# One-hots from tile 54 with a row chunk to each pair, and gelus and gates moved in larger pieces, in the expert stage of a hybrid decoder step

## The reference, cut to what matters

```python
def one(xb):
    qh = (xb @ wq).reshape(PEER_BLOCK, PEER_HEADS, 2, PEER_DQ // 2)
    s1 = jnp.einsum('nhd,kd->nhk', qh[:, :, 0], subkeys[0])
    s2 = jnp.einsum('nhd,kd->nhk', qh[:, :, 1], subkeys[1])
    v1, i1 = lax.top_k(s1, PEER_TOPK)
    v2, i2 = lax.top_k(s2, PEER_TOPK)
    cand = v1[..., :, None] + v2[..., None, :]
    sc, ci = lax.top_k(cand, PEER_TOPK)
    e = i1[ci // 16] * 128 + i2[ci % 16]
    g = jax.nn.softmax(sc, axis=-1)
    a = jax.nn.gelu(jnp.einsum('nd,nhkd->nhk', xb, u[e]))
    return jnp.einsum('nhk,nhkd->nd', g * a, v[e])
```

## Time and profile before

| | us |
|---|---|
| median of 3 runs (lowest to highest) | 2361.18 (2359.29 to 2371.97) |
| the profiled execution's own time | 2364.91 |
| its span | 2363.3 |
| PE busy | 2133.0 (90%) |
| DVE busy | 1359.9 (58%) |
| POOL busy | 546.1 (23%) |
| ACT busy | 360.4 (15%) |
| U pass, first product to last group | 955.0 to 1619.6 |
| V pass, first product to last | 1632.5 to 2244.8 |

### The profile page before, as it was taken

The page is one execution under the profiler, slowest core; times in us unless marked ns, Lnnn a source line. Parts: engine busy times, 40 slices in busy tenths (PEclk is TensorE's granted clock), DMA queues, the critical chain, the costliest instruction groups (busy, mean ns, idle before and its releaser), DMA issues. The chain is left out here.

```text
span 2363.3 us, 24834 instructions
## 1 busy us (share of the span) xinstructions
PE 2133.0 (90%) x8879; PEld 1588.1 (67%) x8879; DVE 1359.9 (58%) x2817; ACT 360.4 (15%) x743; POOL 546.1 (23%) x516
## 2 busy tenths in 40 slices
PE   6958989967999989999769999997998999989997
PEld 4745677735888857677557777775666666666776
DVE  2006477752463089699997777775555455555432
ACT  1001156630010101211111221221000000000011
POOL 1001000031000000332343333333344354444200
PEclk9979999976579999999989999998999999999998
DMA  3151131032032422788689999898999999999721
GB/s 124 48 92 44 61 107 45 27 86 93 27 123 72 143 97 81 283 270 294 233 290 347 356 330 361 331 358 319 346 354 343 345 383 378 382 338 356 259 93 42
DMA packets 210225, 511.84 MB, mean 217 GB/s; under 512 B 19789, under 2 KB 106453, under 8 KB 208438
## 3 DMA queue, kind: packets, MB, share of 16 engines
q1 hardware_dynamic: 146358, 294.72, 36.0%
q0 software_dynamic: 60288, 213.96, 24.2%
q10 hardware_dynamic: 3456, 1.57, 0.2%
HBM read 460.45 MB, written 49.72 MB: 216 GB/s over the span
## 5 line engine op out<-in xcount | busy, mean ns | idle before, releaser
L1892 PE MATMUL ex_ps<-proj,ex_ring 128*128 128x320 f32 x2048 | 570.7, 442 | 54.5 <-DMA ex_ring<-in_v 54.5
L1837 PE MATMUL ex_ps<-h,ex_ring 128*128 128x320 f32 x2048 | 570.2, 435 | 8.5 <-DMA ex_ring<-in_uT 8.5
L1892 PEld LDWEIGHTS ex_ps<-proj,ex_ring 128*128 128x128 f32 x2048 | 397.5, 195 | 227.4 <-DMA ex_ring<-in_v 60.2
L1837 PEld LDWEIGHTS ex_ps<-h,ex_ring 128*128 128x128 f32 x2048 | 385.2, 191 | 160.1 <-DMA ex_ring<-in_uT 9.7
L2054 DVE TENSOR_TENSOR proj<-proj 128x320 f32<-128x320 f32 x128 | 54.4, 487 | 289.5 <-DMA proj<-scratch_a 267.1
L1999 DVE SCALAR_TENSOR_TENSOR gx_sum<-proj,gx_sum 128x1024 f32<-128x1024 f32 x120 | 154.1, 1284 | 8.4
L1745 POOL DMA_INDIRECT scores<-in_u,at_last x26 | 30.7, 1182 | 502.7 <-POOLq L1496 407.9
L1981 DVE CUSTOM_DVE_ANT_0 proj<-proj,gx_tokens 128x1024 f32<-128x1024 f32 x120 | 143.6, 1221 | 2.9 <-DMA proj<-in_u,at_upper 2.6
L1745 POOL DMA_INDIRECT proj<-in_u,at_last x76 | 87.7, 1154 | 195.6 <-DVE proj L1981 181.3
L379 PE MATMUL gate_ps<-h,work 128*128 128x260 f32 x512 | 120.6, 390 | 3.3 <-DMA work<-in_w_t 3.3
L1926 ACT ACTIVATE proj<-proj 128x2 f32<-128x2 f32 x100 | 20.4, 204 | 671.9 <-DVE proj L1981 671.8
(11 more groups left out here) (370 smaller groups left out, 2803.3 us busy)
## 6 DMA issues: line engine op xcount, KB each, us to landing
ex_ring<-in_uT SPq DMA_DIRECT2D x128, 512.0 KB, 5.7
ex_ring<-in_v SPq DMA_DIRECT2D x128, 512.0 KB, 7.8
scratch_a<-ex_gelu SPq DMA_DIRECT2D x128, 160.0 KB, 5.7
scratch_w<-proj SPq DMA_DIRECT2D x10, 2048.0 KB, 10.9
proj<-scratch_a SPq DMA_DIRECT2D x32, 640.0 KB, 12.9
proj<-scratch_w SPq DMA_DIRECT2D x32, 640.0 KB, 14.3
work<-in_w_t SPq DMA_DIRECT2D x37, 512.0 KB, 3.6
mg_ring<-in_w_q SPq DMA_DIRECT2D x32, 512.0 KB, 3.4
```

What stands on the lines that cost most here:

```text
L1837: last = nc.tensor.matmul(y[:, bank(n), 0:TD], u[:, n % UR, k, :], xn[:, k, 0:TD], start=(k == 0), stop=(k == DC - 1))
L1892: last = nc.tensor.matmul(y[:, m, 0:TD], ring[:, (E1 + e) % UR, m * P:(m + 1) * P], H[e // EG % 2][:, e % EG, :], start=(e == 0), stop=(e ...
```

## The change

The one-hots start at tile 54, and 80 groups are spread over 74 tiles (six tiles carry two), with one chunk of rows to each pair of groups, so 40 chunks beside the groups and 46 in the V pass. `scratch_a` is laid out by partition. ACT itself stores gelus, two tiles to a store. SP in the U pass waits for PE's product and for nothing of ACT's; it stores a block one tile later than it is full. Gelus and gates are loaded in parts: the first of 4 tiles, 15 of 8, the last of 4. The first part's gates are loaded as eight blocks of ten before the U pass ends, and the other two blocks are read by DVE from staging. Two gate slots and one gelu slot now lie in `st`.

```diff
-    PER_TILE = 1
-    W0 = E1 - NG // PER_TILE
+    W0 = 54
     TURN = W0 - 1
-    EG = 4
-    NE = E1 // EG
+    EG = 8
+    HEAD = 4
+    parts = [(0, HEAD)] + [(e, min(e + EG, E1)) for e in range(HEAD, E1, EG)]
+    LATE = NWB - 2
-    W_EVERY = 5
-    U_CHUNKS = PRE_CHUNKS + 2 * (NG // W_EVERY)
+    U_CHUNKS = PRE_CHUNKS + NG // 2
+    def groups_to(n):
+        return 0 if n < W0 else (n - W0 + 1) * NG // (E1 - W0)
-    DOTS_AT += [W0 + W_EVERY * (i // 2) + (3 if i % 2 else 1) for i in range(U_CHUNKS - PRE_CHUNKS - 1)]
+    DOTS_AT += [tile_of(2 * i + 1) for i in range(U_CHUNKS - PRE_CHUNKS - 1)]
...
+        st_h, st_w, st_more = views(st, (EG * TD,) * 3)
+        H_at, w_at = [small, st_h], [st_more, st_w]
...
             def load_hidden(g):
-                sp.dma_start(H[g % 2], A_dram[g * EG:(g + 1) * EG].rearrange("e p n -> p e n")).then_inc(s_hl[g % 2], 16)
+                e0, e1 = parts[g]
+                sp.dma_start(hidden_of(g), A_dram[:, e0:e1, :]).then_inc(s_hl[g % 2], 16)
+            def store_weights(g0, g1):
+                for b in range(g0 * GT // WB, g1 * GT // WB):
+                    sp.wait_ge(s_wc, (b + 1) * WB // GT)
+                    sp.dma_start(W_dram[b], staged[:, b % 2].rearrange("p i n -> p (i n)")).then_inc(s_ws[b % 2], 16)
...
-                sp.wait_ge(s_ge, n + 1)
-                sp.dma_start(A_dram[n], ge[:, n % UR, :]).then_inc(s_as[n % UR], 16)
-                done = (n - W0 + 1) * PER_TILE * GT
-                if n >= W0 and done % WB == 0:
-                    b = done // WB - 1
-                    sp.wait_ge(s_wc, done // GT)
-                    sp.dma_start(W_dram[b], staged[:, b % 2].rearrange("p i n -> p (i n)")).then_inc(s_ws[b % 2], 16)
+                store_weights(groups_to(n - 2), groups_to(n - 1))
                 if n == E1 - UR:
-                    for r in range(UR):
+                    for r in range(2):
                         sp.wait_ge(s_as[r], 16)
+                        sp.wait_ge(s_ws[r], 16 * (LATE // 2))
                     load_hidden(0)
-            for r in range(2):
-                sp.wait_ge(s_ws[r], 16 * (NWB // 2))
-            load_weights(0)
+                    load_weights(0)
             for e in range(UR):
                 sp.wait_ge(s_pu, E1 - UR + e + 1)
                 load_v(e)
-            for r in range(UR):
-                sp.wait_ge(s_as[r], 16 * (E1 // UR))
+            store_weights(groups_to(E1 - 2), NG)
+            for r in range(2):
+                sp.wait_ge(s_as[r], 16 * (E1 // 4))
+            for r in range(2):
+                sp.wait_ge(s_ws[r], 16 * (NWB // 2))
+            sp.wait_ge(s_h, HEAD)
             load_hidden(1)
             load_weights(1)
+            load_weights(2)
             for e in range(E1):
                 if e + UR < E1:
                     sp.wait_ge(s_pv, e + 1)
                     load_v(e + UR)
-                g = e // EG
-                if e % EG == 0 and g + 2 < NE:
-                    sp.wait_ge(s_h, (g + 1) * EG)
+                g = part_of[e]
+                if g >= 1 and e == parts[g][0] and g + 2 < len(parts):
+                    sp.wait_ge(s_h, parts[g][1])
                     load_weights(g + 2)
-                if e % EG == EG - 1 and g + 2 < NE:
+                if e + 1 == parts[g][1] and g + 2 < len(parts):
                     load_hidden(g + 2)
...
             def gelu(n):
                 act.wait_ge(s_pu, n + 1)
                 if n >= UR:
-                    act.wait_ge(s_as[n % UR], 16 * (n // UR))
+                    act.wait_ge(s_as[n // 2 % 2], 16 * (n // 4))
                 nc.scalar.activation(ge[:, n % UR, :], y[:, bank(n), 0:TD], ACT.Gelu).then_inc(s_ge, 1)
+                if n % 2:
+                    act.wait_ge(s_ge, n + 1)
+                    act.dma_start(A_dram[:, n - 1:n + 1, :], ge[:, n % UR - 1:n % UR + 1, :]).then_inc(s_as[n // 2 % 2], 16)
...
-                if g % W_EVERY in (0, 2):
+                if g % 2 == 0:
                     dot(chunk + 1)
-                elif g % W_EVERY in (1, 3):
+                else:
                     add(chunk)
                     chunk += 1
...
+                if g == 0:
+                    dve.wait_ge(s_wc, NG)
...
+                        nc.vector.tensor_tensor(h[:, 0:LATE], h[:, 0:LATE], weights_of(g)[:, :, e, :], ALU.mult)
+                        nc.vector.tensor_tensor(h[:, LATE:NWB], h[:, LATE:NWB],
+                                                staged[:, :, :, :].rearrange("p b i n -> p b (i n)")[:, :, e * WB:(e + 1) * WB],
+                                                ALU.mult).then_inc(s_h, 1)
...
-                while chunk < U_CHUNKS + (NC - U_CHUNKS) * (g + 1) // NE:
+                while chunk < U_CHUNKS + (NC - U_CHUNKS) * (quad + 1) // (E1 // HEAD):
...
-               "A": nc.dram_tensor("scratch_a", [E1, P, TD], F32).ap(),
+               "A": nc.dram_tensor("scratch_a", [P, E1, TD], F32).ap(),
```

More of the change, by code:

```diff
@@ L1642, in experts @@
     NG = TD // GT
-    PER_TILE = 1
-    W0 = E1 - NG // PER_TILE
+    W0 = 54
     TURN = W0 - 1
     WIDE = TURN - 4
-    EG = 4
-    NE = E1 // EG
+    EG = 8
+    HEAD = 4
+    parts = [(0, HEAD)] + [(e, min(e + EG, E1)) for e in range(HEAD, E1, EG)]
+    part_of = {e: g for g, (e0, e1) in enumerate(parts) for e in range(e0, e1)}
+    LATE = NWB - 2
     GR = 5
@@ L1655, in experts, with tile_of @@
     PRE_CHUNKS = 14
-    W_EVERY = 5
-    U_CHUNKS = PRE_CHUNKS + 2 * (NG // W_EVERY)
+    U_CHUNKS = PRE_CHUNKS + NG // 2
+    def groups_to(n):
+        return 0 if n < W0 else (n - W0 + 1) * NG // (E1 - W0)
+    def tile_of(g):
+        return next(n for n in range(W0, E1) if groups_to(n) > g)
     def tile_at(us):
@@ L1677, in experts @@
         A, B = (flat[:, i * 2 * GT * P:(i + 1) * 2 * GT * P].rearrange("p (q t n) -> p q t n", q=2, t=GT) for i in range(2))
-        st, small, rest, turned, rows3, dh = views(scratch, (2 * P * WB, 2 * EG * TD, 3 * PH * PK * 2 + 3 * 64, 3 * TD, 3 * 2 * D, 2 * STEPS))
+        st, small, rest, turned, rows3, dh = views(scratch, (2 * P * WB, EG * TD, 3 * PH * PK * 2 + 3 * 64, 3 * TD, 3 * 2 * D, 2 * STEPS))
         staged = st.rearrange("p (b i n) -> p b i n", b=2, n=WB)
@@ L1681, in experts, with hidden_of, weights_of @@
         s8a = st[:, DC * P:DC * P + PH * TS].rearrange("p (h b) -> p h b", h=PH)
-        H = [t[:, 0:EG * TD].rearrange("p (e n) -> p e n", e=EG) for t in (small, st)]
-        w = [t[:, EG * TD:2 * EG * TD].rearrange("p (k e n) -> p k e n", k=NWB, e=EG) for t in (small, st)]
+        st_h, st_w, st_more = views(st, (EG * TD,) * 3)
+        H_at, w_at = [small, st_h], [st_more, st_w]
+        def hidden_of(g):
+            e0, e1 = parts[g]
+            return H_at[g % 2][:, 0:(e1 - e0) * TD].rearrange("p (e n) -> p e n", n=TD)
+        def weights_of(g):
+            e0, e1 = parts[g]
+            if g == 0:
+                return small[:, HEAD * TD:HEAD * TD + LATE * HEAD * WB].rearrange("p (k e n) -> p k e n", k=LATE, e=HEAD)
+            return w_at[g % 2][:, 0:(e1 - e0) * TD].rearrange("p (k e n) -> p k e n", k=NWB, n=WB)
         dots, hid = dh[:, 0:STEPS], dh[:, STEPS:2 * STEPS]
@@ L1692, in experts @@
         s_u = [a.sem(f"ex_tile_loaded{r}") for r in range(UR)]
-        s_as = [a.sem(f"ex_gelu_stored{r}") for r in range(UR)]
+        s_as = [a.sem(f"ex_gelus_stored{r}") for r in range(2)]
         s_hl = [a.sem(f"ex_hidden_loaded{r}") for r in range(2)]
@@ L1783, in load_hidden @@
             def load_hidden(g):
-                sp.dma_start(H[g % 2], A_dram[g * EG:(g + 1) * EG].rearrange("e p n -> p e n")).then_inc(s_hl[g % 2], 16)
+                e0, e1 = parts[g]
+                sp.dma_start(hidden_of(g), A_dram[:, e0:e1, :]).then_inc(s_hl[g % 2], 16)
             def load_weights(g):
-                sp.dma_start(w[g % 2].rearrange("p k e n -> p k (e n)"),
-                             W_dram[:, :, g * EG * WB:(g + 1) * EG * WB].rearrange("k p c -> p k c")).then_inc(s_wl[g % 2], 16)
+                e0, e1 = parts[g]
+                k = LATE if g == 0 else NWB
+                sp.dma_start(weights_of(g).rearrange("p k e n -> p k (e n)"),
+                             W_dram[0:k, :, e0 * WB:e1 * WB].rearrange("k p c -> p k c")).then_inc(s_wl[g % 2], 16)
+            def store_weights(g0, g1):
+                for b in range(g0 * GT // WB, g1 * GT // WB):
+                    sp.wait_ge(s_wc, (b + 1) * WB // GT)
+                    sp.dma_start(W_dram[b], staged[:, b % 2].rearrange("p i n -> p (i n)")).then_inc(s_ws[b % 2], 16)
             for n in range(UR):
@@ L1881, in _ @@
                         pe.wait_ge(s_xc, ND + 1)
-                    for _ in range(PER_TILE):
+                    while g < groups_to(n):
                         weights(g)
@@ L1892, in _ @@
                     last = nc.tensor.matmul(y[:, m, 0:TD], ring[:, (E1 + e) % UR, m * P:(m + 1) * P],
```

(25 more changed lines are left out.)

## The result

The changed kernel takes 2291.93 us (four runs, 2290.41 to 2294.8) against 2360.23 for the kernel before, a ratio of 0.9688 with a 95% interval of 0.9649 to 0.9728; measured again on another chip 2292.66, 0.9695 (0.9665 to 0.9725). The forecast was 2307 (2278 to 2340), faster at 0.88. The direction and the range hold; the gain is 68 us (73 in the second measurement) where the sum said 54.

The account below looks back on a forecast made before the run. DVE's picking bound the turn, PE the U pass, DMA the V pass; the change would make the U pass DMA-bound. -3 (U pass) and -51 (V pass) took 2364.9 to 2311, or 2307 in terms of the median; range 2278 to 2340.

Parts of the forecast that it names:

- The turn: Start of the expert stage: six tiles, 25.9 us of work, fill PE's 27.6 us wait for DVE's last pick.
- The groups and chunks on DVE: U pass beside the groups: 40 pairs with chunks cost DVE 372 us, under PE's 386, so DVE does not bind.
- The U pass on DMA: Beside the groups: eight extra chunks bring DMA work to 409 us over PE's 386, pass ends at 1617, -3 us.
- (b): Rival: DMA does not bind; U pass ends at 1594, V pass takes 559 us, total 2269; chance 0.09.
- the share of 0.98 or more: Sign that the forecast is right: DMA share beside the groups, with PE there at 94 to 97%, not 100%.
- The step to the V pass: Between last group and first V product: gap falls from 13 to 2 us, -11; new stall and slow clock, +10.
- The new stall at tile 4: Early V pass: `v` tile 4 lands late behind the last block and three 1.31 MB pieces; 8 us (2 to 14).
- The rest of the V pass: DMA demand for four tiles falls from 110% to 98%; `v` stalls shrink from 60.5 to 10 us; V pass -51.
- The sum: Whole kernel: -3 for the U pass and -51 for the V pass give -54 us, 2311 from 2364.9.
- (a): Rival: the byte rate, 360 GB/s from 1208 on, is the ceiling; 2331 us in all; chance 0.14.
- (c): Rival: DVE late in the U pass through slow gathers; pass ends at 1644, +24, total 2334; chance 0.07.
- (d): Rival: larger pieces stop `v` tiles at each of 15 part borders, 6.4 us each; slower, 2390; chance 0.06.

Follow-up runs that it names:

- e3: Changed kernel with one-hots from tile 48 and the old chunk rule, so only stores and loads differ from the kernel before: 2334.09 us, ratio 0.9889.
- e4: Changed kernel with the old chunk rule (two chunks to five groups) put back, all else kept: 2310.34 us, ratio 0.9787.
- e1: Kernel before with only the one-hots moved to start at tile 54; chunks, stores and loads as before: 2344.44 us, ratio 0.9930.
- e11: Changed kernel with 37 more loads of 512 KB beside the groups, into memory that nothing reads: 2321.43 us, ratio 0.9819.
- e2: Kernel before with only one chunk to each pair of groups, so 46 chunks in the V pass for 54: 2335.95 us, ratio 0.9886.
- e5: Changed kernel with parts of four tiles all through, gates in 512-byte packets again, twice the loads: 2315.98 us, ratio 0.9791.
- e7: Changed kernel with no chunk in the V pass's first sixteen tiles, its 46 chunks shared over the other 28 fours: 2296.13 us, ratio 0.9703.
- e8: Changed kernel with v tile 4 issued ahead of SP's wait for the last blocks, and no chunk in the first four fours: 2289.50 us, ratio 0.9667.
- e9: As e8, but chunks paced at 46 to 32 fours, the last six behind DVE's last product; against the kernel before: 2278.42 us, ratio 0.9641.

## Why the prediction was right, and where its sum was off

**The turn** was right: six tiles went into the wait of 27.6 us, and the U pass is 23.2 us shorter for it (e3 to e4). The claim beside it, that PE does not lack `u` tiles once SP is free of the gelus, was right too: with the gelus PE waits 9.4 us for one (e1). Its price is smaller than that wait, 2.5 us of the pass's length, because the changed kernel has 7.4 us of waits at the turn where I had about 2. PE runs ahead until ACT, which stands for the last pick, must empty a bank for it; this I had not seen.

**The groups and chunks on DVE** were right. DVE is busy 350 of 386 us, and beside the groups PE waited for it once, for the first group (3.6 us). Even in e11 it falls behind only through its gathers.

**The U pass on DMA** is the step that failed: "DMA-bound", 409 us, -3. PE's own 386 us held, which was rival (b) for this half. Of my signs for it, the share of 0.98 or more came (1.01), but PE was at 100% and not at 94 to 97%, and the last group came at 1594.6, named there as the sign of (b). So not only a size was off: the chunks did not make DMA the limit of this pass, and e2, which has the chunks alone, says the same. The DMA queues from 1208 to 1620 in the kernel before, then from 1208 to 1594 in the kernel after:

```profile
q1 hardware_dynamic: 24136, 72.30, 48.0%
q0 software_dynamic: 18749, 68.24, 43.8%
```

```profile
q0 software_dynamic: 22825, 83.12, 54.7%
q1 hardware_dynamic: 12522, 56.65, 37.8%
q10 hardware_dynamic: 5184, 11.80, 7.7%
```

With 0.2% for instructions that is 1.004 x 386 = 388 us of work for 151.9 MB, 2.55 us per MB. Before it was 379 us for 140.8 MB, 2.69 per MB, and I had carried the work over as if each byte would cost the same. The sum of bytes was good: 140.8 - 4.1 + 16.8 = 153.5 MB. By queue, the gathers (q0) added 31 us, for 7.5 chunks in the stretch, where I had 44 for eight, and SP's and ACT's queues fell by 22 where I had 14.

That work of 388 us, and not the ceiling, is most of the miss: at a share of 1.00 it would have ended the pass 2 us behind PE's own end, while my 409 us would have taken 397 even at the 1.03 of the earlier trace rows. The ceiling was not 1.00 either: e11 held 1.03 and 414 GB/s, at which 153.5 MB take 371 us, under PE's 386.

Why a byte costs less of the engines' time in the fuller pass is only in part the number of packets (24136 of SP's queue before, 17706 of SP's and ACT's after, 4 us at my 9.8 ns). The rounded share over the rate from 1208 to 1594 in each run says as much. With the old pace of the chunks it is 2.68 us per MB in e1, with the small pieces, and 2.70 and 2.67 in e3 and e4, with the large ones. With the chunks added it is 2.59 in e2, which has the small pieces, 2.57 in the changed kernel, and 2.48 with the extra loads of e11. So it goes with the load and hardly with the pieces; why, these runs leave open.

**The step to the V pass.** The gap of 2 us was right (2.4). The new stall at tile 4 was named, with its place and its cause, at 8 (2 to 14); it was 11.1. What was mis-sized is the block ahead of it: SP stood 15.2 us for it and not the 6.3 of before, when no gather ran. A second stall of 7.3 us at tile 9 was not in the sum. With the tiles that ran slower behind the waits (granted clock 0.87 from 1594 to 1670) that makes 18.4 us of waits and some 5 more in place of 10.

**The rest of the V pass.** Taken at 10 us of stalls, measured none. The demand in four tiles orders most of the runs, with the waits for `v` behind tile 9:

| | chunks to a four | asked | parts | later waits, us |
|---|---|---|---|---|
| before, e1 | 1.69 | 110% | 4 | 41.5, 42.9 |
| e2 | 1.44 | 102% | 4 | 19.8 |
| e5 | 1.44 | 101% | 4 | 19.8 |
| e3, e4 | 1.69 | 106% | 8 | 13.8, 16.7 |
| e7, e8 | 1.64 | 105% | 8 | 9.8, 11.2 |
| after, e9 | 1.44 | 98% | 8 | 0, 0 |

Within either size of parts more demand means more waiting (e2 and e5 are alike), and the changed kernel stands just under 100%. The prices in the column "asked" are my estimates, but the traces bear them out here: the queues' shares of the 400 us from 1700 to 2100, over the fours that PE did in its busy time, make 18.3, 18.0 and 17.2 us for before, e4 and e5, where I had 19.0, 18.3 and 17.4. But parts of eight at 106% wait less than parts of four at 101%. So the larger pieces do more than save packets, and my estimate of 9.8 ns a packet covers only that. What it is besides (a `v` tile late by the burst at each border, or DVE stopped twice as often by a load) these runs don't tell.

**The sum.** The U pass ended 22 us earlier than forecast, the V pass took 4 more (14 more at the start, 10 less later): -54 - 22 + 4 = -72, and -73.4 was measured, the rest behind the V pass. That the V pass came within 4 us is luck in part, for its two errors have opposite signs. The total stayed in the range because the range had PE's own end of the U pass (-26) among its ends. For the V pass the mechanism ran as described and its sizes were off; for the U pass I had the wrong engine as the limit.

**The rivals.** (a), a byte rate of 360 GB/s as the ceiling, has fallen: 393 GB/s over the U pass, 414 in e11. The Trainium skill's figure of about 358 GB/s for transfers between HBM and SBUF ("SBUF — State Buffer", summary of rules for kernel authors) does not bind one core alone here; the measurement decides. (b) held for the U pass, not for the start of the V pass. (c) did not come: PE's one wait for one-hots was 3.6 us. (d), stalls at each of the 15 borders, did not come: there is one, at the border of parts 0 and 1, and a second inside part 1. (Its own terms give 2393, not 2390.)

## What to carry to other kernels

Where two stages lean on different resources, work with transfers of its own can move from the one that is short of DMA to the one that is short of PE, up to the point at which a tile asks for as much DMA time as PE time; count that per stage, not over the kernel. Take the ceiling from a stretch in which the engines had no pause, or make one with extra loads, and don't carry the work per byte of an emptier stage over to a fuller one: here it fell from 2.69 to 2.55 us per MB. And an engine's queue that waits for another engine's result passes on its waits: see what each wait in it holds up before filling an idle stretch, and take its worth from the length of the stage, not from the one wait that goes (9.4 us went here, 2.5 were gained).

## What the runs showed of the hardware

One core held 414 to 417 GB/s between HBM and SBUF for 294 us, at a DMA share of 1.03, from three queues at once (e11); the profile's share does go over 1. Only shorter stretches had more: 1.04 at 404 GB/s from 1594 to 1633 in the changed kernel.

Moving the gelu stores from SP to ACT paid by a wait, not by the time of issuing. The Trainium skill ("DMA: Bandwidth & Descriptors", issuing engines are not separate DMA queues) says that DMAs started by several engines save only the sequencer's time to start them. Whether the bandwidth stays the same no run here can show: e4, with the stores on ACT, and e1, with them on SP, move 356 and 354 GB/s beside the groups, but PE is the limit there and the bytes are the same. What changed is that the wait for the gelu left SP's list with the store, and with it a stall of 9.4 us (e1) and 2.5 us of the U pass. e1 and the changed kernel differ in the size of the stores too, so that this is the cause is read from the traces, and not tested alone.
